# Attention in pairs of maps with three-product scores, and the conditioning moved from TensorE to GpSimd: one Trainium2 core

## The reference

```
h = rms_norm(x, attn_norm) @ w_in
MLA:  6 heads, q and k of 96 features (64 + 32 rotated), v of 64, from normed latents of 384 and 256
diff: 4 heads of two maps, q and k of 64, v of 128
      o = softmax(q1 k1') v - lam * softmax(q2 k2') v, rms_norm per head, times a gain
GQA:  6 query heads, 2 key and value heads of 64, two-axis rotary positions
x = x + concat(o_mla, o_diff, o_gqa) @ w_o
x = x + (silu(y @ w_gate) * (y @ w_up)) @ w_down,   y = rms_norm(x, ffn_norm)
```

## Time and profile before

| | |
|---|---|
| median of the runs | 3343.29 us (3342.02 to 3347.43) |
| the profiled execution | 3349.31 us |
| its span | 3347.5 us |
| chain of work that ended last, by engine | PE 89%, DVE 5%, ACT 4%, issue 1%, DMA 1% |
| mean granted clock of TensorE | 0.958 of full speed |
| busy: PE, DVE, ACT, POOL | 3173.7, 1123.2, 994.6, 280.1 us |
| first layer's stretch from the end of its projections to w_o | 192.5 to 500.5 us |
| second layer's | 1120.7 to 1418.2 us |
| most of the first layer's FFN | 598 to 879 us |

### The profile page before, as it was taken

The page is one execution under the profiler, slowest core; times in us unless marked ns, Lnnn a source line. Parts: engine busy times, 40 slices in busy tenths (PEclk is TensorE's granted clock), DMA queues, the critical chain, the costliest instruction groups (busy, mean ns, idle before and its releaser), DMA issues.

```text
span 3347.5 us, 35084 instructions
## 1 busy us (share of the span) xinstructions
PE 3173.7 (95%) x14020; PEld 2217.0 (66%) x14020; DVE 1123.2 (34%) x1827; ACT 994.6 (30%) x1607; POOL 280.1 (8%) x268
## 2 busy tenths in 40 slices
PE   7999999999989999999999999979899899989997
PEld 6866564788878765647888665544566544468886
DVE  2624340433236243414332313342533300043322
ACT  3354451222233544512222133332222200022222
POOL 4371000000023520000000000000000000000000
PEclk7989999999989998999999899989999899989998
DMA  4221120333322211113323311000111132123331
GB/s 106 80 72 39 51 76 25 101 91 87 95 68 78 86 37 51 60 46 100 100 81 92 94 38 38 26 27 26 51 38 51 26 75 76 50 76 101 87 93 60
DMA packets 340274, 221.98 MB, mean 66 GB/s; under 512 B 8364, under 2 KB 334892, under 8 KB 340112
## 3 DMA queue, kind: packets, MB, share of 16 engines
q1 hardware_dynamic: 337360, 214.65, 22.1%
q0 software_dynamic: 2224, 2.99, 0.9%
q10 hardware_dynamic: 528, 2.10, 0.2%
HBM read 217.62 MB, written 2.10 MB: 66 GB/s over the span
## 4 chain that ended last, share of the span: by engine, by line
PE 89%; DVE 5%; ACT 4%; issue 1%; DMA 1%; DVEq 0%; ACTq 0%; SPq 0%
PE ps L591 83%; PE ps L602 4%; PE ps L618 2%; DVE R L1693 1%; ACT R L1206 1%; DVE xL L1689 0%; DVE x_lows L1689 0%; DMA ident<-in_c_ident 0%; PE ps L945 0%; DMA R<-in_ctx 0%; ACT R L1202 0%; ACT L1195 0%; DVE R L1782 0%; DVE R L1764 0%; DVE wL L1715 0%
## 5 line engine op out<-in xcount | busy, mean ns | idle before, releaser
L591 PE MATMUL ps<-R 128*128 128x64 f32 (+6 forms) x2272 | 497.2, 371 | 29.3 <-ACT R L1206 8.7
L591 PEld LDWEIGHTS ps<-R 128*128 128x128 f32 (+3 forms) x2272 | 298.1, 192 | 225.4 <-issue 133.4
L591 PE MATMUL ps<-xH,wH 128*128 128x512 f32 x1056 | 416.8, 395 | 22.0 <-DVE xL L1689 22.0
L1206 ACT ACTIVATE R<-ps 128x512 f32<-128x512 f32 (+9 forms) x504 | 248.4, 493 | 567.2 <-PE ps L591 502.6
L591 PE MATMUL ps<-xL,wH 128*128 128x512 f32 x1056 | 413.7, 392 | 0.0
L591 PE MATMUL ps<-xH,wL 128*128 128x512 f32 x1056 | 413.6, 392 | 0.0
L591 PE MATMUL ps<-U,ring 128*128 128x512 f32 (+5 forms) x960 | 401.8, 573 | 12.3 <-ACT R L1412 12.3
L1356 ACT ACTIVATE wH<-raws 128x2048 fp32r<-128x2048 f32 (+1 forms) x114 | 192.9, 1692 | 568.2 <-PE ps L591 567.6
L591 PEld LDWEIGHTS ps<-U,ring 128*128 128x128 f32 (+2 forms) x960 | 181.1, 192 | 209.3 <-issue 183.4
L591 PE MATMUL ps<-R,ring 128*128 128x512 f32 x704 | 311.6, 594 | 2.9 <-DVE R L1932 1.6
L1715 DVE TENSOR_TENSOR wL<-raws,wH 128x2048 fp32r<-128x2048 f32 (+1 forms) x114 | 229.3, 2011 | 233.2 <-ACT wH L1356 226.4
(11 more groups left out here) (279 smaller groups left out, 3296.4 us busy)
## 6 DMA issues: line engine op xcount, KB each, us to landing
raws<-in_w_gate_up SPq DMA_DIRECT2D x88, 512.0 KB, 5.1
ring<-in_w_in SPq DMA_DIRECT2D x36, 1024.0 KB, 6.1
ring<-in_w_ada SPq DMA_DIRECT2D x24, 1024.0 KB, 5.2
raws<-in_w_down SPq DMA_DIRECT2D x32, 704.0 KB, 4.6
raws<-in_w_ffn_in SPq DMA_DIRECT2D x44, 512.0 KB, 5.0
ring<-in_w_in SPq DMA_DIRECT2D x34, 512.0 KB, 5.6
raws<-in_w_ffn_out SPq DMA_DIRECT2D x16, 704.0 KB, 4.6
ring<-in_w_o SPq DMA_DIRECT2D x5, 1280.0 KB, 5.8
```

Source lines behind the costliest of these rows:

```text
L591: return nc.tensor.matmul(o, a, b, start=first, stop=last)
L1206: ap.do(f(dst, src, ACT.Copy), sem)
```

## The change

**Attention.** `attend` becomes a loop over pairs of maps: 16 diff pairs (both maps of a head for one token tile), 12 GQA and 12 MLA pairs (two heads), 40 in a layer. Scores are three fp32r products for each map; for diff and GQA the two maps stand on the two row halves. A pair's scores fill one of two buffers of two banks (`SP[a % 2]`); exponentials write one of three `PX` buffers. For diff, DVE combines the two maps (p0 + ratio * p1, the ratio holds -lam and both row sums) ahead of one bank of transposes and four value matmuls. For GQA and MLA, POOL multiplies both maps by their inverse row sums (`weigh`, 128x1024), PE fills two banks of transposes, and the value matmuls give the transposed output of two heads on the two column halves; no output transposes are left for these.

**q and k.** They are transposed as 24 items, four ahead of the first pair and 20 beside the pairs, one in each of 20 rounds (`BESIDE`); ACT takes the high part, DVE the low part of each.

**Order.** W_IN becomes diff q and k, gqa q (192, 192), gqa k and v, latents, diff v. POOL's rotation of gqa now stands between the low parts from the ninth piece on, after a wait (`gqa_inv_ready`), while DVE rotates diff q and k. PE waits `bT_ready` after the first piece of diff v.

**Conditioning.** It leaves the attention for the FFN: 64 items (32 in a layer, one beside each of the FFN's pieces 5 to 36), each 512 KB loaded by SP, one POOL multiplication of 128x1024 and three additions (512, 256, 128), one fp32 matmul of one column and one small ACT copy. 32 MB are loaded in place of 24. The pieces of w_o come as three DMAs each.

The core of the diff (lines of only "..." mark what is left out):

```diff
+        N_DIFF, N_PAIR = BH * TT, (BH + GH // 2 + AH // 2) * TT
+        FAMILY = ["diff"] * N_DIFF + ["gqa"] * (GH // 2 * TT) + ["mla"] * (AH // 2 * TT)
+
+        BESIDE = {-2: ["dq0", "dk0"], -1: ["dq1", "dk1"], 2: ["dq2"], 3: ["dk2"], 6: ["dq3"], 7: ["dk3"],
+                  9: ["gk"], 10: ["gq0"], 12: ["gq1"], 13: ["gq2"],
+                  17: ["mq0"], 19: ["mk0"], 21: ["mq1"], 23: ["mk1"],
...
+        ITEM_BANK = ([D_BANKS[0], D_BANKS[1]] * 2 + [A_BANKS[1], D_BANKS[1]] * 4
+                     + [D_BANKS[1] for item in ITEMS if item[0] == "m"])
...
+        PX = [spare[:, 0, :].rearrange("p (a c) -> p a c", a=2), spare[:, 1, :].rearrange("p (a c) -> p a c", a=2), Pb]
+        PT = [PTb, SQ[:, :, 0:512]]
+
+
+
+        ADA = [(m, 0) for m in range(16)] + [(m, 1) for m in range(16)] + [(m, 0) for m in range(16, 48)]
+        ADA_FIRST, N_ADA = 5, len(ADA) // L
 
...
+        W_IN = (quarter_pieces("diff_qk", c1, 2 * BH * BV)
+                + [("gqa_q", G0, GH // 2 * GD), ("gqa_q", G0 + GH // 2 * GD, GH // 2 * GD), ("gqa_kv", G0 + GH * GD, 2 * GK * GD)]
+                + quarter_pieces("latent", 0, c1)
+                + quarter_pieces("diff_v", c1 + 2 * BH * BV, BH * BV))
+        L_PIECES = [len(W_IN) + 2 + len(WO[l]) for l in range(L)]
...
+            def weigh(l, p_):
+
+                a = l * N_PAIR + p_
+                r = 2 * (a % 8)
+                pg.more(sums_inverted)
+                pg.do(nc.gpsimd.tensor_tensor(PX[a % 3], PX[a % 3], bc(rinv[:, r:r + 2], S, 2), ALU.mult), weighted)
+
+            def output_norm(l, t):
+
+                o = O[:, t, :].rearrange("p (h d) -> p h d", h=BH)
+                pg.do(nc.gpsimd.tensor_tensor(o, o, bc(ssO[:, t, :], BV, 2), ALU.mult))
+                pg.do(nc.gpsimd.tensor_tensor(o, o, bc(gO[:, l, :], BH, 1), ALU.mult), o_ready)
+
+            def conditioning(l):
+
+                pool.wait_ge(cs_ready, 1)
+                for a in range(l * N_ADA, (l + 1) * N_ADA):
+                    w = ada_half(a)
+                    pool.wait_ge(ada_in[a % 2], 16 * (a // 2 + 1))
+                    w_ = w.rearrange("p (k c) -> p k c", k=KT)
+                    pg.do(nc.gpsimd.tensor_tensor(w_, w_, bc(cvec[:, :, ADA[a][1]], P, 2), ALU.mult))
+                    for n_ in (4, 2, 1):
+                        pg.do(nc.gpsimd.tensor_tensor(w[:, 0:n_ * P], w[:, 0:n_ * P], w[:, n_ * P:2 * n_ * P], ALU.add),
+                              ada_summed if n_ == 1 else None)
 
...
+                    if j == 8:
+                        pg.more(gqa_inv_ready)
+                    if j >= 9:
+                        rotate(pg, nc.gpsimd, j - 9, Tg, rsG, gtmp, 8, GD, gG, ropeG, gT_ready, l, 6, True)
+                rotate(pg, nc.gpsimd, 3, Tg, rsG, gtmp, 8, GD, gG, ropeG, gT_ready, l, 6, True)
...
+                for p_ in range(N_DIFF, N_PAIR):
+                    weigh(l, p_)
+                    if p_ in OUTPUT_NORM_AT:
+                        if p_ == OUTPUT_NORM_AT[0]:
+                            pg.more(diff_inv_ready)
+                        output_norm(l, OUTPUT_NORM_AT.index(p_))
+                conditioning(l)
...
+            def modulation(a):
+
+                pe.wait_ge(ada_summed, a + 1)
+                if a >= 1:
+                    pe.wait_ge(ada_read, a)
+                mm(SP[1][:, 1, 0:1], ada_half(a)[:, 0:P], ones[:, 0:1], True, True).then_inc(ada_full, 1)
...
+                def scores(p_):
+                    a, t = first + p_, p_ % TT
+                    if a >= 2:
+                        pe.wait_ge(s_exp, a - 1)
+                    pe.wait_ge(qk_ready, done + items_needed(p_))
+                    q_k, o, tok = pair_items(p_), SP[a % 2], slice(t * P, (t + 1) * P)
+                    if len(q_k) == 1:
+                        (qh, ql), (kh, kl) = [ITEM_SLOTS[item] for item in q_k[0]]
+                        for n, (q, k) in enumerate(((qh, kh), (qh, kl), (ql, kh))):
+                            for c in range(2):
+                                r = slice(c * BD, (c + 1) * BD)
+                                ins = mm(o[:, c, :], QKP[r, q, tok], QKP[r, k, :], n == 0, n == 2)
+                    else:
+                        for c in range(2):
+                            (qh, ql), (kh, kl) = [ITEM_SLOTS[item] for item in q_k[c]]
+                            for n, (q, k) in enumerate(((qh, kh), (qh, kl), (ql, kh))):
+                                ins = mm(o[:, c, :], QKP[0:AQK, q, tok], QKP[0:AQK, k, :], n == 0, n == 2)
...
+                def probabilities(p_):
+                    a = first + p_
+                    if FAMILY[p_] == "diff":
+                        pe.wait_ge(combined, l * N_DIFF + p_ + 1)
+                    else:
+                        pe.wait_ge(weighted, l * (N_PAIR - N_DIFF) + p_ - N_DIFF + 1)
+                    for c in range(1 if FAMILY[p_] == "diff" else 2):
+                        bank = A_BANKS[c]
+                        pe.wait_ge(*released[id(bank)])
+                        for s_ in range(TT):
+                            ins = nc.tensor.transpose(bank[:, s_ * P:(s_ + 1) * P], PX[a % 3][:, c, s_ * P:(s_ + 1) * P], ident[:, :])
+                        ins.then_inc(pt_full, 1)
+                        released[id(bank)] = (pt_act, a + 1) if c == 0 else (pt_dve, l * (N_PAIR - N_DIFF) + p_ - N_DIFF + 1)
...
+                def values(p_):
+                    a, i, t = first + p_, p_ // TT, p_ % TT
+                    pt = PT[a % 2]
+                    pe.wait_ge(pt_act, a + 1)
+                    if FAMILY[p_] == "diff":
+                        bank = D_BANKS[0]
+                        pe.wait_ge(*released[id(bank)])
+                        group(None, bank[:, 0:BV], [(pt[:, 0, s_ * P:(s_ + 1) * P], V[:, s_, VB + i * BV:VB + (i + 1) * BV])
+                                                    for s_ in range(TT)]).then_inc(v_full, 1)
+                        released[id(bank)] = (v_done, v0 + p_ + 1)
+                        return
+                    n = (p_ - N_DIFF) // TT
+                    bank = D_BANKS[0]
+                    pe.wait_ge(pt_dve, l * (N_PAIR - N_DIFF) + p_ - N_DIFF + 1)
+                    if t == 0:
+                        pe.wait_ge(*released[id(bank)])
+                    for s_ in range(TT):
+                        for c in range(2):
+                            at_ = VG + c * GD if FAMILY[p_] == "gqa" else VA + (2 * (i - BH - GH // 2) + c) * AV
+                            ins = mm(bank[c * AV:(c + 1) * AV, t * P:(t + 1) * P], V[:, s_, at_:at_ + AV],
+                                     pt[:, c, s_ * P:(s_ + 1) * P], s_ == 0, s_ == TT - 1)
+                    if t == TT - 1:
+                        ins.then_inc(ot_full, 1)
+                        released[id(bank)] = (ot_done, ot0 + n + 1)
+
+                def diff_outputs(f):
+                    bank = D_BANKS[1]
+                    pe.wait_ge(*released[id(bank)])
...
+                scores(0)
+                scores(1)
+                for p_ in range(N_PAIR + 4):
+                    if p_ + 2 < N_PAIR:
+                        scores(p_ + 2)
+                    if p_ >= 4:
+                        values(p_ - 4)
+                    if 2 <= p_ < N_PAIR + 2:
+                        probabilities(p_ - 2)
+                    beside(p_)
+                    if p_ in DIFF_OUTPUTS_AT:
+                        diff_outputs(DIFF_OUTPUTS_AT.index(p_))
+                for bank in (*A_BANKS, D_BANKS[1]):
+                    pe.wait_ge(*released[id(bank)])
+                assert db.n % 2 == 1
 
...
+                    if what == "diff_v" and a == V_AT:
+                        pp.more(bT_ready, TT)
+                        for item in BESIDE[-2]:
+                            part_transposes(l, item, (d_free, db.n))
+                for n, item in enumerate(BESIDE[-1]):
...
+                    if ada_at(l, q) is not None:
+                        modulation(ada_at(l, q))
...
+                def exponentials(p_):
+                    a = first + p_
+                    act.wait_ge(s_max, a + 1)
+                    if p_ >= 3:
+                        act.wait_ge(pt_full, pt0 + banks_filled(p_ - 2))
+                    for c in range(2):
+                        n = 2 * (a % 8) + c
+                        ap.do(f(PX[a % 3][:, c, :], SP[a % 2][:, c, :], ACT.Exp, bias=nmax[:, n:n + 1], accum_out=rsum[:, n:n + 1]),
+                              s_exp if c == 1 else None)
+
+                def transposed(p_):
+                    act.wait_ge(pt_full, pt0 + banks_filled(p_) + 1)
+                    ap.do(f(PT[(first + p_) % 2][:, 0, :], A_BANKS[0][:, :], ACT.Copy), pt_act)
+
+                def diff_output(p_):
+                    h, t, r = p_ // TT, p_ % TT, 2 * ((first + p_) % 8)
+                    act.wait_ge(v_full, l * N_DIFF + p_ + 1)
+                    ap.do(f(O[:, t, h * BV:(h + 1) * BV], D_BANKS[0][:, 0:BV], ACT.Copy, scale=rinv[:, r:r + 1]), v_done)
...
```

(46 more changed lines are left out.)

489 lines of the change are left out of this document (234 added, 255 removed), and 1 row of the table BESIDE.

## The result

The changed kernel takes 3366.01 us, the median of 4 runs (3358.4 to 3369.95), against 3345.14 for the kernel before in the same comparison: a ratio of 1.0047, 95% interval 1.0035 to 1.0060. The forecast was slower, 3417, in a range of 3290 to 3490. So the side and the range held, but the change of time was forecast at 74 us and came to 21. The profiled execution takes 3365.0 us, its span is 3363.2.

A forecast was written before the change was run, and what follows sets the result against it. TensorE was taken to bound the kernel before. 3349.3 - 95.5 (attention) - 4.6 (w_o) + 45 (collision) + 16 (FFN conditioning) = 3310, as a median 3304; +113 for the low clock gave 3417 us, range 3290 to 3490.

The forecast's parts named there:

- The collision: Projections: POOL's gqa rotation and VectorE's diff rotation take turns, TensorE waits 25 and 20 us; +45.
- The low clock: Attention rounds: idle time lets TensorE's clock fall; half taken between ends 0 and +226, so +113.
- The closed chain: Attention rounds: ACT and TensorE take turns; rounds 212 us a layer, drain and output banks 7; -53 and -42.5 by layer.
- the clock holds: Rival for the 40 rounds: under 0.3 of them at the low clock, 3304 to 3372 us; chance 0.27.
- that of the forecast: Main case: clock low for 0.3 to 0.7 of the rounds, 3372 to 3462 us; chance 0.42.
- Conditioning in the FFN: FFN: 64 one-column matmuls at 0.20 us, each with a hand-over of 0.05; +16 us.
- w_o: First w_o tile after attention: no longer waits for output banks, 11.0 us against 8.69; -4.6 in both layers.
- What bounded the kernel before: Attention: TensorE busy 296.34 of 308.0 us, so every instruction taken off it is time while it stays last.
- no collision: Rival for the projections: no collision on DVE, -45, 3372 us; chance 0.08.
- halves don't run at once: Rival for attention: row and column halves don't run beside each other, 40 us a layer more, 3497; chance 0.06.
- Each engine a round behind the other: Rival for attention: no closed chain, TensorE's 130 us in place of 212, -164, 3140 us; chance 0.03.

The follow-up runs named there:

- copies_first: Changed kernel with TensorE's scores after values and transposes, and ScalarE's bank copy and scaled output before the exponentials, item's high part behind: 3178.39 us, ratio 0.9495.
- the filled rounds: Changed kernel with six unread fp32r matmuls behind the transposes of rounds 2 to 17: 3365.33 us, ratio 1.0041; filled_plain limits them to rounds without an item.
- vector_copies_first: copies_first with POOL's gqa rotation after VectorE's, and VectorE's copies of second transposed bank and finished head pair before the next rowmax: 3116.36 us, ratio 0.9308.
- before_eighth: Kernel before, with one matmul in place of eight in each of the 24 conditioning pieces, loads and copies kept: 3378.97 us, ratio 1.0095.
- gqa_conditioning_kept: before_eighth, but the four conditioning pieces in the GQA units keep their eight matmuls: 3312.82 us, ratio 0.9894 to the kernel before.
- filled_plain: Changed kernel with six unread matmuls behind the transposes of diff rounds that have no item: 3340.25 us, ratio 0.9983.

## Why the forecast was right in its side and wrong in its size

Two terms of the sum failed, both by their size. The collision was put at +45 us, and the projections became 19.4 us longer. The low clock was put at +113 and cost some 98, by the estimate below; its rounds had a chain of which one link was wrong. By the steps of the sum, against the profiled execution (3423 forecast, 3365 measured, 58 less):

- **The closed chain: right in kind.** ScalarE and TensorE take turns in every round, and the copies_first run shows that this costs 185 us, the low clock that goes with it included. One link was put wrong, in the diff rounds at the high clock. I had TensorE's scores between the exponentials and the values; there the values wait for the bank that the scaled output frees, behind ScalarE's copy (0.61 and 0.38 in the chain above), and the scores run beside these. The round is longer than I said, 4.45 for a plain one in place of 4.15. MLA's chain is the one of the forecast, with the scores in it, and its length was near, 5.47 against 5.27:

```profile
490.76 0.69 ACT L1395 ACTIVATE spare<-scores,R 128x512 f32<-128x512 f32 x1 [4.78 <-PE ps L831]
...
492.41 1.66 PE L704 MATMUL scores<-QK_parts 96*128 96x512 f32 x6 [1.32 <-ACT spare L1395]
...
494.00 1.10 PE L704 MATMUL ps<-R 128*64 128x128 f32 x16
...
495.02 1.09 PE L831 MATMUL ps<-ident,R 128*128 128x128 f32 x8
...
496.23 0.69 ACT L1395 ACTIVATE R<-scores,R 128x512 f32<-128x512 f32 x1 [2.62 <-PE ps L831]
```

- **The clock: right in share, too dear by its price.** I took half of the rounds at the low clock. The trace has 135 of 255 us from the first exponential to the last in the first layer (0.53) and 130 of 254 in the second (0.51): for diff 0.67, GQA 0.50 and MLA 0.40 in the first. No row had led to one half, it was a choice between the ends 0 and 226, so that it came out is luck in part. The price failed. I multiplied all of TensorE's work in a round by 1.87, 2.11 us more for a plain diff round. Measured are 6.27 against 4.45, 1.82 more, because at the high clock ScalarE's 0.99 stands where the scores stand at the low one. An MLA round with 3.4 us at the low clock took 7.01, 1.54 more than at the high clock. From such rounds I put the clock's cost at some 98 us (an estimate: diff 17, GQA 19, MLA 14 in the first layer, 48 in the second), 15 less than the 113. The rounds and the drain together came to 265.5 and 264.0 us where the sum had 212 + 7 + 56.5 = 276 each: 22 us of the 58; the 7 that the clock leaves over are not attributed. By its number the measured time lies in the band of "the clock holds" (3304 to 3372) and by its low share in that of the forecast (0.3 to 0.7), so the number alone would have named the wrong case. The rule of the Trainium skill ("TensorE: Matmul & The Clock Gate", section "A second HAM failure mode: psum-queue depth-cycling"), that short idle times in each cycle make the clock go up and down, agrees with the diff pairs' 0.67 and with the filled rounds.
- **The collision: right in kind, too dear by more than twice.** VectorE's and POOL's operations do take turns, but the projections became 13.1 + 6.3 us longer, not 25 + 20, and of the 13.1 some 2 us are another wait. VectorE's rotation was ready at 191, not 206: its 40 operations took 51 us from 140 on, 13.3 of them beside three low parts (3.32, 4.99 and 5.00) and 38 for the other 37 operations. Alone the 37 would take 27 us, so POOL's rotation added 11, where I had added all of its 25. In the trace a pair of operations takes less than both, 1.42 us (from 151.08 to POOL's next at 152.50) for POOL's 0.99 alone (in the kernel before) and VectorE's 0.69. In the second layer TensorE waited for the result for just 4.4 us. This is the largest part of the miss, 26 us. The rule of the Trainium skill ("SBUF — State Buffer", section "SBUF: two separate sides"), that the two shut each other out for a whole instruction, agrees with the rows of 151 and 157 us; in the FFN, where by it the sum would have gone towards 61 more, TensorE lost no more than the next point says.
- **Conditioning in the FFN: right.** 16 forecast; the two FFNs took 376.5 us in place of 369.1 each, 14.8 in all, that is 0.23 for each of 64 items, where a matmul and a hand-over had been put at 0.25.
- **w_o: right in kind.** 6.1 us less, 4.6 forecast. What lies between the projections and the first exponential took 39.5 and 30.2 us where 35.6 was put for each, 1.5 less in all. The second block, 0 forecast, took 6 us less; as it varies by 10 between kernels in which it is the same, no cause is to be sought in the change. So 6 of the 58 us may be chance.
- **What bounded the kernel before: wrong.** "Every instruction taken off TensorE is time" doesn't hold: seven eighths of the conditioning cost less than nothing, because those in the GQA units brought the clock back; with these kept, 53 us of the others gave 36. The sum didn't use the sentence, as it replaced the whole stretch. The 0.44 us that the forecast calls the price of changing the array's rows compares a diff unit with an MLA unit, and their values differ in width too (128 and 64 columns); a GQA unit, with 64, has 2.09 in place of 2.14 there, so 0.39.

Of the rivals, "the clock holds" is out (share 0.53 low), "no collision" and "halves don't run at once" too: TensorE's busy time in vector_copies_first, 133 us, is near the 130 that the price with halves side by side gave, and not the 170 of halves one after the other. "Each engine a round behind the other" became true only with the orders changed.

## What to carry to other kernels

When a change lets engines work behind each other over rings of buffers, write down for one round which instruction each engine's next one waits for and in which place of its own queue the releasing one stands; here the order of a few calls in the loops of three engines was worth some 230 us, with the same rings and the same operations, and changed on TensorE alone only some 22. On each engine put what frees a buffer for others (copies out of a bank) ahead of what has to wait for fresh data. And before work is taken off TensorE, look at the granted clock around it: the work may be what keeps the rest at full speed.

## What the runs showed of the hardware that was not expected

- TensorE ran for 100 us at a granted clock of 0.50 while it was busy for 40.00 of 40 us, in units of fp32 matmuls on 64 rows with transposes between them (before_eighth). With four pieces of eight full-row matmuls kept there (gqa_conditioning_kept) it was back at 1.00 after 13.7 us, 2.3 us behind the start of the one piece that stood in the low stretch. What of them does it, rows, columns or their number, was not tried.
- Filling idle time with six matmuls of no use in seven rounds of a layer made the kernel 21 us faster (filled_plain against the change, by the ratios).
